# V transposed inside the second projection, the last keys' chain moved into it, and weight loads placed behind x loads, in a one-core hybrid streaming encoder kernel

## The chip, the cores and the metric

The kernel runs on one core of a Trainium2 chip. The metric is the device time of one execution in microseconds (us); lower is better. Engines: TensorE (PE in the profile, its weight loads PEld), VectorE (DVE), ScalarE (ACT), GpSimd (POOL) and SyncE (SP), which here issues nearly all DMAs.

## The reference

One inference step of a two-layer encoder on 2048 prompt tokens and 64 sample tokens, width 1024, in float32:

1. Layer A: x is RMS-normalised and projected to an x branch and a SiLU gate; a causal convolution of width 4, two block-diagonal gates, a linear recurrence over time, the product with the gate, an output projection, and the residual sum x1.
2. Shared keys and values: `kv = rmsnorm(x1) @ w_kv`, 128 columns of keys (2 heads of 64, RMS-normalised per head) and 128 of values.
3. Layer B: x1 is normalised and projected to 1024 query columns (16 heads, RMS-normalised per head) and 1024 gate columns (SiLU). Each chunk of 64 tokens attends to itself and the two chunks before it (the sample: to a cache of 128 tokens and itself), with a learned sink per head. The result times the gate goes through an output projection and is added to x1.

Keys and values of the last 128 tokens, and the convolution's and the recurrence's states, are outputs too.

## The kernel before

**Number format.** Each float32 matmul is three matmuls of rounded operands (high times high, low times high, high times low), so weights and inputs are split into a high part (ACT, `high_part` L906, `high_input` L405) and a low part (`low_part` L911 on DVE or POOL, `low_input` L418 on DVE). Activations lie with features in partitions and tokens in columns.

**Stages.** (a1) first projection, 6 steps of 352 tokens. (recurrent) 8 steps of 264 tokens (RN = 8, RT = 264), each of 4 turns; PE does gates L1432, output projection `out` L1453 (matmul L1465), keys and values L1448, the token sum L1472 and the key sum L1418. (b1) second projection, steps s = 1 to 6 (PN = 6) of PT = 352 tokens, each of 16 slots j of 24 matmuls L791: j < 8 give a block of queries, j >= 8 a block of gates. (attention) a sample tile and 8 tiles of 256 tokens (AN = 8), 8 units each; the first 8 units run inside the last 8 slots of b1 (a `late` slot).

**A slot of b1.** On DVE the block is read out of PSUM (`evacuate`, L691). For a query block ACT squares it (L554) into one of two buffers q2, and DVE adds it to qacc (copy L642 for the first block, sum L645 after), one slot later. After slot 8 PE sums qacc over the heads (`head_sum` L767, matmul L773), and it waits there for the eighth sum (q2_added). The same slots prepare the next step's input: ACT L405 and L412 (square), DVE L418 and L431. In step 1 each slot also splits a weight unit: ACT L906, then POOL L911. SP issues, in the order of the slots, input loads L392, weight loads `load_unit` L843 and the stores of finished gate and query blocks L481 and L485 (`project_sync` L444). Each engine runs its list in order, so whatever is issued behind a waiting instruction waits too.

**What hangs on slots.** `project_sync` has a table of extra work by (step, slot), run at the slot's start: (1,4) `store_memory` L1046, the last K and V blocks to DRAM; (1,12) `store_states` L1584, ten small stores; (PN,0) `start` L1599, which waits for all query stores and loads the sample tile and tile 1 (`tile` L1547); (PN,8) and (PN,10) gate loads; (PN,12) to (PN,15) tile 2.

**The last keys.** The chain for the last 264 tokens runs in b1's first slots: DVE L1256 and L1258 read keys and values out, DVE L1261 squares, PE `key_sum` L1414 (L1418, after slot 0), ACT root L1360, DVE reciprocal L1265 and product L1267. ACT's first square of step 1 waits for that key sum (`r.kms_done`), and so does POOL before `spread_heads` L963 at slot 1. All token and key sums use PSUM bank 5, so `out` blocks 1 and 3 wait for the roots that read it.

**V in attention.** Values are kept with features in partitions, but PE needs them with tokens in partitions. So each tile loads `m.vt` by DMA (L1556, L1557, L1571), and in unit 0 PE transposes it (`transpose_v` L1708: four blocks L1720, then L1722 and L1723), and ACT and DVE copy the result to `m.v` and `m.v_last` (`read_v`, L1963 to L1972 on ACT, L1839 on DVE). The transposes of probabilities (`transpose_p` L1693, matmuls L1702 and L1705) use the same banks 4 and 5 and wait for those copies.

```python
            def head_sum(t):
                eng.wait_ge(m.q2_added, NB * (t + 1))
...
                if i == 0:
                    eng.wait_ge(m.va_done, s + 1)
                    eng.wait_ge(m.vb_done, s + 1)
```

Of the kernel before, what the change touches and what calls it, by code (L numbers as in the profile page):

```python
# [24 lines left out]
P = 128  # L25
D = 1024
# [61 lines left out]
def build(nc, A):  # L88
    stack = ExitStack()
    with stack:  # L90
# [50 lines left out]
        spread_made = sem("spread_made")  # L141
# [21 lines left out]
        def project_memory(tag, heads):  # L163
            with ExitStack() as own:
# [28 lines left out]
                if heads:  # L193
                    b(f"{tag}_gap0", [P, 2048 - 3 * PT])
                    m.q2, m.qacc = b(f"{tag}_q2", [P, 2, PT]), b(f"{tag}_qacc", [P, PT])
                else:
                    m.std = b(f"{tag}_std", [P, PT])
# [19 lines left out]
            if heads:  # L217
                m.late_tanh, m.late_done = sem(f"{tag}_late_tanh"), sem(f"{tag}_late_done")
                m.q2_done, m.q2_added = sem(f"{tag}_q2_done"), sem(f"{tag}_q2_added")
                m.qms_done = sem(f"{tag}_qms_done")  # L220
# [86 lines left out]
        with ExitStack() as own:  # L307
# [24 lines left out]
            m.vt = [b(f"m_vt{i}", [P, WINDOW + AT]) for i in range(2)]  # L332
            m.v = [b(f"m_v{i}", [P, 4, P]) for i in range(2)]
            b("m_gap1", [P, 23 * PT - 7424 + 32])
# [28 lines left out]
        m.vt_done = sem("m_vt_done")  # L363
        m.va_done = sem("m_va_done")
        m.vb_done = sem("m_vb_done")
# [4 lines left out]
        m.v_last_zero = sem("m_v_last_zero")  # L370
# [73 lines left out]
        def project_sync(eng, m, starts):  # L444

            def body(s, par):
                for j in range(2 * NB):
# [20 lines left out]
                    if known(s, 1, PN):  # L468
                        t = s - 1
                        if m.heads and not gate:  # L470
                            continue
# [66 lines left out]
        def project_scalar(eng, m, after):  # L538
            def body(s, par):
# [97 lines left out]
        def add_query(eng, m, t, q):  # L637

            eng.wait_ge(m.q2_done, NB * t + q + 1)
            if q == 0:  # L640
                need(eng, m.qms_done, t)
                nc.vector.tensor_copy(m.qacc[:, :], m.q2[:, 0, :]).then_inc(m.q2_added, 1)  # L642
            else:
                eng.wait_ge(m.q2_added, NB * t + q)
                nc.vector.tensor_tensor(m.qacc[:, :], m.qacc[:, :], m.q2[:, q % 2, :], ALU.add).then_inc(m.q2_added, 1)  # L645
# [120 lines left out]
        def project_tensor(eng, m, after):  # L766
            def head_sum(t):  # L767

                if isinstance(t, int) and t == 0:
                    eng.wait_ge(spread_made, 2)  # L770
# [192 lines left out]
        def spread_heads(eng):  # L963
# [5 lines left out]
              .then_inc(spread_made, 1)  # L969
            eng.wait_ge(spread_made, 1)  # L970
            nc.gpsimd.affine_select(out=spread, in_=spread, compare_op=ALU.is_ge, fill=0.0, base=NB - 1,
                                    pattern=[[NB, P // NB], [0, NB]], channel_multiplier=-1).then_inc(spread_made, 1)
# [40 lines left out]

        EARLY = {(PN, 2): 0, (PN, 6): 1, (PN, 8): 2, (PN, 11): 3, (PN, 13): 4}

# [36 lines left out]
        def recurrent_sync(eng):  # L1052
# [31 lines left out]

            def load_next(pair, q):
# [4 lines left out]
            def body(s, par):  # L1090
                for g in range(NG):
# [79 lines left out]
            for i in range(2):  # L1171
                eng.wait_ge(r.x1_stored[i], 16 * RN * NB // 2)

        def recurrent_vector(eng):
# [73 lines left out]
            def tail_read(t):  # L1248
# [10 lines left out]
                eng.wait_ge(r.kv_read, 2 * t + 1)  # L1259
                need(eng, r.kms_done, t)  # L1260
                nc.vector.tensor_tensor(r.k2[:, :], r.k[:, :], r.k[:, :], ALU.mult).then_inc(r.k2_done, 1)  # L1261

            def tail_norm(t):
                eng.wait_ge(r.kstd_done, t + 1)
                nc.vector.reciprocal(r.std[:, :], r.std[:, :]).then_inc(r.krec_done, 1)  # L1265
                eng.wait_ge(r.krec_done, t + 1)
                nc.vector.scalar_tensor_tensor(out=r.k[:, :], in0=r.k[:, :], scalar=vec[:, KN, 0:1], in1=r.std[:, :],  # L1267
                                               op0=ALU.mult, op1=ALU.mult).then_inc(r.k_done, 1)

            def turn(s, par, g):  # L1270
# [13 lines left out]
                if known(s, 2, RN + 1) and g == 3:  # L1284
                    tail_norm(s - 2)
# [28 lines left out]
            eng.wait_ge(r.x1_free, 1)  # L1314

        def recurrent_scalar(eng):
# [29 lines left out]
            def turn(s, par, g):  # L1346
# [5 lines left out]
                if known(s, 2, RN + 1) and g == 2:  # L1352
                    eng.wait_ge(r.ms_done, t + 1)
                    need(eng, r.k_done, t)
                    nc.scalar.activation(r.std[:, :], bank[5][:, 0:RT], ACT.Sqrt, scale=1.0 / D,
                                         bias=eps[:, 0:1]).then_inc(r.std_done, 1)
                if known(s, 2, RN + 1) and g == 3:
                    eng.wait_ge(r.rstd_done, t + 1)
                    eng.wait_ge(r.kms_done, t + 1)
                    nc.scalar.activation(r.std[:, :], bank[5][:, 0:RT], ACT.Sqrt, scale=1.0 / HEAD,  # L1360
                                         bias=eps[:, 0:1]).then_inc(r.kstd_done, 1)
# [52 lines left out]
        def key_sum(eng, t, last):  # L1414
            eng.wait_ge(r.k2_done, t + 1)
            if not last:
                eng.wait_ge(r.resid_done, NB * (t + 1) + 2)
            nc.tensor.matmul(bank[5][:, 0:RT], head_ones[:, :], r.k2[:, :], start=True, stop=True)\  # L1418
              .then_inc(r.kms_done, 1)

        def recurrent_tensor(eng):
# [31 lines left out]
            def out(t, tp, blk):  # L1453
# [3 lines left out]
                if blk == 1:  # L1457
                    need(eng, r.std_done, t)
                if blk == 3:
# [9 lines left out]
            def token_sum(t):  # L1469
                eng.wait_ge(r.sq_added, NB * (t + 1))  # L1470
                eng.wait_ge(r.resid_done, NB * (t + 1))
                nc.tensor.matmul(bank[5][:, 0:RT], ones[:, :], r.acc[:, :], start=True, stop=True)\  # L1472
# [72 lines left out]

        def attention_sync(eng):
            def tile(s, par, parts=range(4)):  # L1547

                done = m.tile_loaded[par]
                if isinstance(s, int) and s == 0:  # L1550
# [5 lines left out]
                    eng.dma_start(m.vt[0][:, 0:WINDOW], A["v0"]).then_inc(done, 16)  # L1556
                    eng.dma_start(m.vt[0][:, WINDOW:WINDOW + SAMPLE], A["v"][:, 0:SAMPLE]).then_inc(done, 16)  # L1557
# [7 lines left out]
                for part in parts:  # L1565
# [4 lines left out]
                    if part == 1:  # L1570
                        eng.dma_start(m.vt[par][:, w0:w0 + width], A["v"][:, cols(at - WINDOW + w0, width)])\  # L1571
                           .then_inc(done, 16)
# [26 lines left out]
            def start():  # L1599
# [4 lines left out]
                for stored in b1.stored:  # L1604
                    eng.wait_ge(stored, 16 * NB)
                tile(0, 0)
                tile(1, 1)

            def gate_sample():
                eng.wait_ge(b1.proj_done, 2 * NB * (PN - 1) + NB - 1)  # L1610
                tile_gate(0, 0)

            def gate_first():
                eng.wait_ge(b1.qms_done, PN)
                tile_gate(1, 1)
# [17 lines left out]
            project_sync(eng, b1, {(1, 4): lambda: store_memory(eng, RN - 1), (1, 12): store_states, (PN, 0): start,  # L1633
# [32 lines left out]
        def loaded(eng, s, par):  # L1666

            eng.wait_ge(m.tile_loaded[par], s * 56 + (112 if par == 0 else 56))
# [5 lines left out]
        def attention_tensor(eng):  # L1674
# [18 lines left out]
            def transpose_p(s, par, i):  # L1693
# [4 lines left out]
                if i == 0:  # L1698
                    eng.wait_ge(m.va_done, s + 1)
                    eng.wait_ge(m.vb_done, s + 1)  # L1700
# [7 lines left out]
            def transpose_v(s, par):  # L1708

                before = unit_of(s, 0)  # L1710
                need(eng, m.pta_done, before)
                need(eng, m.ptb_done, before)
                loaded(eng, s, par)
                if isinstance(s, int) and s == 0:
# [450 lines left out]
```

## Time and profile before

| | us |
|---|---|
| three runs | 1519.57, 1520.12, 1522.78 |
| their median | 1520.12 |
| profiled execution, device time | 1520.08 |
| span of its profile | 1518.3 |
| PE busy in the span | 1469.9 (97%) |
| DVE, ACT, POOL busy | 1042.4, 709.0, 258.1 |
| mean granted TensorE clock, share of full speed | 0.993 |

The span is the part of the execution that the profile covers, on its only core. A time in a row, such as 774.79, is counted in us from the start of the span. A bracket at the end of a row, as `[4.06 <-ACT m_pt_a L1961]`, says how long the engine had been idle before it and what ended that.

### The profile page before, as it was taken

Reading aid. Unit: us, or ns where it says so; the run is one execution under the profiler, and the core shown is the slowest. Engines: PE = TensorE matmul, PEld = TensorE weight load, DVE = VectorE, ACT = ScalarE, POOL = GpSimd, SP = SyncE. Lnnn points to the kernel's source line nnn. Section 1 sums busy time; section 2 is a strip of 40 time slices with the busy share of each in tenths; the row PEclk is TensorE's granted clock in tenths of the full one; section 3 lists DMA queues with packets and bytes.
Section 4 is the critical chain, followed back from the end, with each engine's and each line's share of the span. In section 5 each row is a group of like instructions: output and inputs, shape, how many; then the busy total and the mean of one; then the engine's idle time right before and its main releaser. Section 6 shows DMA issues by size and latency. Waiting matters only on the chain.

```text
span 1518.3 us, 31662 instructions
## 1 busy us (share of the span) xinstructions
PE 1469.9 (97%) x10668; PEld 1409.0 (93%) x10668; DVE 1042.4 (69%) x2254; ACT 709.0 (47%) x1584; POOL 258.1 (17%) x199
## 2 busy tenths in 40 slices
PE   7999999999999999999899999999988999999999
PEld 7999999999899999998899999999976788878888
DVE  7987866765698888888863453534377877767771
ACT  5432432336887777772352341433335444434440
POOL 0011111101344444341440000000001111111110
PEclk9999999999999999999999999999999999999999
DMA  6565655569855555556522202212264244423312
GB/s 238 169 211 198 219 178 202 198 225 334 280 169 171 153 168 163 160 164 209 161 62 81 96 30 91 77 52 92 64 196 130 80 111 121 121 80 102 96 50 77
DMA packets 202711, 219.35 MB, mean 144 GB/s; under 512 B 60496, under 2 KB 189264, under 8 KB 202576
## 3 DMA queue, kind: packets, MB, share of 16 engines
q1 hardware_dynamic: 190448, 208.27, 43.7%
q10 hardware_dynamic: 12128, 9.39, 1.9%
q8 instruction: 71, 1.16, 0.3%
q14 instruction: 64, 0.52, 0.1%
HBM read 132.56 MB, written 85.30 MB: 143 GB/s over the span
## 4 chain that ended last, share of the span: by engine, by line
PE 62%; DVE 5%; ACT 2%; issue 2%; DMA 1%; SPq 0%; ACTq 0%; POOL 0%; DVEq 0%
PE s_banks L791 22%; PE bank L1754 10%; PE bank L1465 10%; PE s_banks L1432 5%; PE s_banks L1687 3%; PE bank L1448 3%; PE bank L791 2%; PE bank L1702 2%; PE bank L1736 2%; ACT m_p L1950 2%; PE bank L1740 1%; DVE m_nmax L1808 1%; PE bank L1705 1%; DMA r_x<-xT_dram 1%; DMA x_dram<-r_x 1%
## 5 line engine op out<-in xcount | busy, mean ns | idle before, releaser
L1950 ACT ACTIVATE m_p<-s_banks,m_nm 128x192 f32<-128x192 f32 (+2 forms) x264 | 106.1, 414 | 185.8 <-DVE m_nm L1812 185.5
L1754 PE MATMUL bank<-m_y_hi,w_hi_a 128*128 128x256 f32 (+1 forms) x512 | 150.7, 294 | 2.8 <-DVE w_lo_a L911 2.1
L1754 PE MATMUL bank<-m_y_lo,w_hi_a 128*128 128x256 f32 (+1 forms) x512 | 145.6, 284 | 0.0
L1754 PE MATMUL bank<-m_y_hi,w_lo_a 128*128 128x256 f32 (+1 forms) x512 | 145.5, 284 | 0.0
L791 PE MATMUL bank<-a_hi,w_hi_a 128*128 128x352 f32 x384 | 123.7, 322 | 1.3 <-DVE a_out L691 1.1
L791 PE MATMUL bank<-a_hi,w_lo_a 128*128 128x352 f32 x384 | 124.0, 323 | 0.0
L791 PE MATMUL bank<-a_lo,w_hi_a 128*128 128x352 f32 x384 | 123.9, 323 | 0.0
L791 PE MATMUL s_banks<-b_hi,w_hi_b 128*128 128x352 f32 x336 | 110.8, 330 | 0.0
L1465 PE MATMUL bank<-r_y_hi,w_hi_a 128*128 128x264 f32 x384 | 109.3, 285 | 0.6 <-ACT r_std L1360 0.6
L1465 PE MATMUL bank<-r_y_lo,w_hi_a 128*128 128x264 f32 x384 | 109.1, 284 | 0.0
L1465 PE MATMUL bank<-r_y_hi,w_lo_a 128*128 128x264 f32 x384 | 108.9, 283 | 0.0
L791 PE MATMUL s_banks<-b_hi,w_lo_b 128*128 128x352 f32 x336 | 108.8, 324 | 0.0
L791 PE MATMUL s_banks<-b_lo,w_hi_b 128*128 128x352 f32 x336 | 108.1, 322 | 0.0
L2007 POOL TENSOR_TENSOR m_y_lo<-m_y,m_y_hi 128x256 fp32r<-128x256 f32 x66 | 48.6, 736 | 349.1 <-DVE m_y_hi L1865 349.1
L578 ACT ACTIVATE a_out_hi<-a_out 128x352 fp32r<-128x352 f32 (+1 forms) x48 | 23.9, 498 | 172.8 <-DVE a_out L745 172.8
L791 PE MATMUL s_banks<-b_hi,w_hi_a 128*128 128x352 f32 x320 | 104.1, 325 | 0.0
L791 PE MATMUL s_banks<-b_hi,w_lo_a 128*128 128x352 f32 x320 | 103.3, 323 | 0.0
L791 PE MATMUL s_banks<-b_lo,w_hi_a 128*128 128x352 f32 x320 | 103.2, 323 | 0.0
L1754 PEld LDWEIGHTS bank<-m_y_hi,w_hi_a 128*128 128x128 f32 x512 | 96.7, 189 | 4.8 <-DVE w_lo_a L911 3.9
L1754 PEld LDWEIGHTS bank<-m_y_lo,w_hi_a 128*128 128x128 f32 x512 | 97.4, 190 | 0.0
L1754 PEld LDWEIGHTS bank<-m_y_hi,w_lo_a 128*128 128x128 f32 x512 | 97.3, 190 | 0.0
L791 PE MATMUL bank<-a_hi,w_hi_b 128*128 128x352 f32 x288 | 93.3, 324 | 0.3 <-DVE a_out L691 0.3
(224 smaller groups left out, 4624.3 us busy)
## 6 DMA issues: line engine op xcount, KB each, us to landing
w_raw_b<-weights_dram SPq DMA_DIRECT2D x26, 512.0 KB, 4.6
w_raw_a<-weights_dram SPq DMA_DIRECT2D x25, 512.0 KB, 4.6
sga_dram<-a_out SPq DMA_DIRECT2D x48, 176.0 KB, 2.9
r_xc_hi<-xc_hi_dram SPq DMA_DIRECT2D x32, 264.0 KB, 3.0
r_xc_lo<-xc_lo_dram SPq DMA_DIRECT2D x32, 264.0 KB, 3.3
r_xc<-xc_dram SPq DMA_DIRECT2D x32, 264.0 KB, 3.8
r_sg<-sga_dram SPq DMA_DIRECT2D x32, 264.0 KB, 3.6
r_x<-xT_dram SPq DMA_DIRECT2D x64, 132.0 KB, 2.1
```

Source lines behind the costliest of these rows:

```text
L578: nc.scalar.activation(m.out_hi[:, q, 0:width], m.out[:, place(m, j), 0:width], ACT.Copy)\
L791: mm = nc.tensor.matmul(project_bank(m, s, j)[:, 0:PT], w[pw][:, kt * P:(kt + 1) * P], x[:, kt, :], start=(n == 0), stop=(n == 3 * NB - 1))
L1432: mm = nc.tensor.matmul(bank[2 * mat + ob][:, 0:RT], w[pw][:, at:at + P], x[px][:, q, kt, :].bitcast(F32R), start=(i == 0), stop=(i == 5))
L1448: mm = nc.tensor.matmul(bank[6 + o][:, 0:RT], w[pw][:, blk * P:(blk + 1) * P], (r.x1_hi, r.x1_lo)[px][:, blk % 2, :], start=(blk == 0 and ...
L1465: mm = nc.tensor.matmul(bank[4 + blk % 2][:, 0:RT], w[pw][:, kt * P:(kt + 1) * P], (r.y_hi, r.y_lo)[px][tp][:, kt, :], start=(i == 0), sto ...
L1687: mm = nc.tensor.matmul(s_banks[:, 2 * (i % 2) + e, bp * 192 + v0:(bp + 1) * 192], m.q[par][rows, j, blk:blk + 2, :].rearrange("p b t -> p ...
L1702: nc.tensor.transpose(bank[4][:, k * P:(k + 1) * P], m.p[:, i % 2, k, 0:P], ident[:, :])
L1705: mm = nc.tensor.transpose(bank[5][:, e * P:(e + 1) * P], last, ident[:, :])
L1736: nc.tensor.matmul(bank[6][e * HEAD:(e + 1) * HEAD, 0:AT], m.v[par][:, j, n * HEAD:(n + 1) * HEAD], m.pt_a[:, e * AT:(e + 1) * AT], start= ...
L1754: mm = nc.tensor.matmul(out_bank(ts, blk)[:, 0:width], w[pw][:, kt * P:(kt + 1) * P], (m.y_hi, m.y_lo)[px][tp][:, kt, 0:width], start=(n = ...
L1950: nc.scalar.activation(m.p[:, q, k, v0:192], s_banks[:, 2 * q + e, bp * 192 + v0:(bp + 1) * 192], ACT.Exp, bias=m.nm[:, q, k:k + 1], accum ...
L2007: nc.gpsimd.tensor_tensor(y_part(m.y_lo, s, par, i), m.y[:, q, :, :], y_part(m.y_hi, s, par, i).bitcast(F32), ALU.subtract).then_inc(m.y_l ...
```

## The change

1. **V is transposed in b1.** V is cut into 18 blocks of up to 128 tokens: the cached one in step 1, four in each of steps 2 to 5, the last 64 tokens in step 6. A block takes four slots: SP reads it (64 KB) into one buffer `v_in`, PE transposes it after the next slot's matmuls (`turn`), ACT copies it to `v_out` in the third, SP writes it to a new DRAM scratch `vt` in the fourth. Steps 2 to 5 do this in slots 4i to 4i+3, step 1 in slots 12 to 15, step 6 in slots 0 to 3. `read_turn` and `write_turn` stand at the end of a slot's work on SP.
2. **Attention reads rows of `vt`.** `m.vt`, `transpose_v`, both `read_v` and the waits on them go. Instead SP loads `m.v` (`values_rows`, 1 to 3 DMAs a tile) and `m.v_last` (`last_rows`, 2 a tile). `start` waits until 17 blocks are written, before its first load; `gate_first` waits for all 18. POOL's memsets are in more pieces.
3. **One q2 buffer.** ACT's square of block j waits for DVE's sum of block j-1; before, of block j-2. ACT's wait on the last key sum goes.
4. **The last keys' chain is spread:** DVE squares after slot 0, PE sums and ACT takes the root after slot 2 (bank 7), DVE reciprocal and product after slot 3, `store_memory` at (1,6). POOL's wait for the key sum stays, ahead of `spread_heads`.
5. **Two sums in free banks.** The token sum of the seventh recurrent block (RN - 2) goes to bank 2 and its key sum to bank 3, so the last `out` no longer waits for the roots.
6. **Weight loads behind x loads.** At recurrent turn (RN, 0), SP issues weight units 1 and 2 of b1 behind the first x load and 3 and 4 behind the second, not all four ahead of both.

```diff
@@ project_sync
+                    else:
+                        read_turn(eng, s, j)
+                        write_turn(eng, s, j)
@@ project_scalar
-                            need(eng, m.q2_added, NB * t + j - 1)
-                            if j == 0 and isinstance(s, int) and s == 1:
-                                eng.wait_ge(r.kms_done, RN)
-                            nc.scalar.activation(m.q2[:, j % 2, :], m.q[:, j, :], ACT.Square)\
-                              .then_inc(m.q2_done, 1)
+                            need(eng, m.q2_added, NB * t + j)
+                            nc.scalar.activation(m.q2[:, :], m.q[:, j, :], ACT.Square).then_inc(m.q2_done, 1)
@@ recurrent_sync
+            def gates_free(s, g, first):
+                if isinstance(s, int) and (s, g) == (RN, 0):
+                    for k in (first, first + 1):
+                        load_unit(eng, U_B1 + k, r.gates_done, 4 * NG * RN)
...
-                    if isinstance(s, int) and (s, g) == (RN, 0):
-                        for k in range(1, 1 + UNITS_GATE):
-                            load_unit(eng, U_B1 + k, r.gates_done, 4 * NG * RN)
...
                     if behind:
                         load_x(behind, 0)
+                    gates_free(s, g, 1)
...
                         load_x(behind, 1)
+                    gates_free(s, g, 3)
@@ recurrent_tensor
-                if blk == 1:
+                if blk == 1 and not last_sums(t - 1):
                     need(eng, r.std_done, t)
-                if blk == 3:
+                if blk == 3 and not last_sums(t - 1):
                     need(eng, r.kstd_done, t)
@@ attention_sync and b1
+        def read_turn(eng, s, j):
+            for i in turns(s, j, 0):
+                n, width = turned(s, i), turn_width(s)
+                need(eng, b1.v_turned, n)
...
+                eng.dma_start(b1.v_in[:, 0:width], src).then_inc(b1.v_read, 16)
+        def turn(eng, s, j):
+            for i in turns(s, j, 1):
+                n, width = turned(s, i), turn_width(s)
+                eng.wait_ge(b1.v_read, n * 16 + 16)
+                need(eng, b1.v_copied, n)
...
+                nc.tensor.transpose(bank[5][0:width, 0:P], b1.v_in[:, 0:width], ident[:, :]).then_inc(b1.v_turned, 1)
+        def copy_turn(eng, s, j):
+            for i in turns(s, j, 2):
...
+                nc.scalar.activation(b1.v_out[0:width, :], bank[5][0:width, 0:P], ACT.Copy).then_inc(b1.v_copied, 1)
+        def write_turn(eng, s, j):
+            for i in turns(s, j, 3):
...
+                eng.dma_start(dst, b1.v_out[0:width, :]).then_inc(b1.v_written, 16)
@@ start
+                eng.wait_ge(b1.v_written, 16 * (4 * (PN - 2) + 1))
                 tile(0, 0)
+                values_rows(0, 0)
                 tile(1, 1)
@@ attention_tensor
-                if i == 0:
-                    transpose_v(s, par)
             def after_queries(s, j):
-                if isinstance(s, int) and (s, j) == (1, 0):
+                turn(eng, s, j)
+                if isinstance(s, int) and (s, j) == (1, 2):
                     key_sum(eng, RN - 1, True)
@@ attention_scalar, unit
-                if i == 0:
-                    read_v(s, par)
```

## Rows read from the trace of the kernel before

**Rows 1.** PE's waits: releaser, us in total, times, longest us.

```profile
PE bank L1448 <- DVE r_x_lo L1233: 8.0, 4, 3.2
PE bank L1720 <- ACT m_pt_a L1961: 7.0, 3, 4.1
...
PE bank L1702 <- ACT m_v_last L1972: 2.7, 5, 0.7
...
PE bank L1465 <- ACT r_std L1360: 0.6, 1, 0.6
...
PE bank L1465 <- ACT r_std L1355: 0.6, 1, 0.6
```

**Rows 2.** PE's timeline, two waits for x: start us, us, instruction [idle].

```profile
697.50 0.39 PE L1448 MATMUL bank<-r_x_hi,w_hi_a 128*128 128x264 f32 x1 [1.61 <-DVE r_x_lo L1233]
...
735.37 0.52 PE L1448 MATMUL bank<-r_x_hi,w_hi_a 128*128 128x264 f32 x1 [3.22 <-DVE r_x_lo L1233]
```

**Rows 3.** The chain that ended last: start us, us, what.

```profile
686.70 7.00 DMA x_dram<-r_x
```

**Rows 4.** PE's timeline at the first head_sum.

```profile
774.79 0.76 PE L773 MATMUL bank<-b_qacc,head_ones 128*128 128x352 f32 x2
```

**Rows 5.** DVE's timeline in b1's step 1.

```profile
746.86 1.16 DVE L1267 SCALAR_TENSOR_TENSOR r_k<-r_k,vec,r_std 128x264 f32<-128x264 f32 x1
...
764.03 1.48 DVE L645 TENSOR_TENSOR b_qacc<-b_qacc,b_q 128x352 f32<-128x352 f32 x1
...
773.99 0.51 DVE L645 TENSOR_TENSOR b_qacc<-b_qacc,b_q 128x352 f32<-128x352 f32 x1
```

**Rows 6.** POOL's timeline in the same stretch.

```profile
744.49 0.40 POOL L967 TENSOR_SCALAR_AFFINE_SELECT head_ones<-ones 128x128 f32<-128x128 f32 x1 [1.14 <-PE bank L1418]
...
745.33 7.30 POOL L911 TENSOR_TENSOR w_lo_b<-w_raw_b,w_hi_b 128x1024 fp32r<-128x1024 f32 x3
...
762.73 2.40 POOL L911 TENSOR_TENSOR w_lo_a<-w_raw_a,w_hi_a 128x1024 fp32r<-128x1024 f32 x1 [1.41 <-ACT w_hi_a L906]
```

**Rows 7.** SP's timeline in the same stretch.

```profile
743.43 7.25 SPq L843 DMA_DIRECT2D w_raw_a<-weights_dram  x3
```

**Rows 8.** ACT's timeline, a slot of the same stretch.

```profile
764.15 0.50 ACT L554 ACTIVATE b_q<-b_q 128x352 f32<-128x352 f32 x1 [1.50 <-DVE b_q L691]
...
765.42 1.04 ACT L906 ACTIVATE w_hi_a<-w_raw_a 128x1024 fp32r<-128x1024 f32 x1
```

**Rows 9.** DMA view: KB each, median us from issue to landing.

```profile
sgb_dram<-b_out SPq DMA_DIRECT2D x48, 176.0 KB, 1.9
...
m_q<-qn_dram SPq DMA_DIRECT2D x33, 256.0 KB, 4.4
...
m_k<-k_dram SPq DMA_DIRECT2D x2, 64.0 KB, 2.6
```

**Rows 10.** SP's timeline in slot 12 of step 2.

```profile
855.80 0.98 SPq L485 DMA_DIRECT2D qn_dram<-b_q  x2
```

**Rows 11.** PE's timeline at the end of slot 13 of step 2.

```profile
857.44 0.32 PE L791 MATMUL s_banks<-b_hi,w_hi_a 128*128 128x352 f32 x1
```

**Rows 12.** SP's timeline around slot 12 of step 1.

```profile
789.70 0.45 SPq L1587 DMA_DIRECT2D conv_sample_dram<-halo_sample  x1
...
798.47 0.46 SPq L481 DMA_DIRECT2D sgb_dram<-b_out  x1
```

**Rows 13.** PE's timeline at the end of slot 13 of step 1.

```profile
794.60 0.32 PE L791 MATMUL s_banks<-b_hi,w_hi_a 128*128 128x352 f32 x1
```

**Rows 14.** SP's timeline in `start`, step 6 slot 0.

```profile
1063.09 3.66 SPq L1574 DMA_DIRECT2D m_q<-qn_dram  x4
```

**Rows 15.** PE's timeline at the end of slot 1 of step 6.

```profile
1061.99 0.32 PE L791 MATMUL s_banks<-b_hi,w_hi_b 128*128 128x352 f32 x1
```

**Rows 16.** Windows: busy us by engine (instructions), granted clock, DMA share, GB/s.

```profile
1140.00:1163.00 23.00, 16.70 (x131) 11.69 (x128) 17.75 (x49) 14.75 (x52) 2.89 (x4) 0.85 0.35 114
```

**Rows 17.** PE's timeline, V's transposes in slot 10 of step 6.

```profile
1107.82 1.12 PE L1720 MATMUL bank<-ident,m_vt 128*128 128x128 f32 x4 [4.06 <-ACT m_pt_a L1961]
```

More of the change, by code:

```diff
@@ L219, in project_memory @@
                 m.q2_done, m.q2_added = sem(f"{tag}_q2_done"), sem(f"{tag}_q2_added")
+                m.v_read, m.v_turned, m.v_copied, m.v_written = (sem(f"{tag}_v_{k}") for k in ("read", "turned", "copied", "written"))
                 m.qms_done = sem(f"{tag}_qms_done")
@@ L467, in body @@
                         load_unit(eng, m.unit + 10 + j)
-                    if known(s, 1, PN):
+                    if known(s, 1, PN) and not (m.heads and not gate):
                         t = s - 1
-                        if m.heads and not gate:
-                            continue
                         if late(m, s, j):
@@ L1172, in recurrent_sync, with key_square, key_norm @@
                 eng.wait_ge(r.x1_stored[i], 16 * RN * NB // 2)
+        def key_square(eng, t):
+            eng.wait_ge(r.kv_read, 2 * t + 1)
+            need(eng, r.kms_done, t)
+            nc.vector.tensor_tensor(r.k2[:, :], r.k[:, :], r.k[:, :], ALU.mult).then_inc(r.k2_done, 1)
+        def key_norm(eng, t):
+            eng.wait_ge(r.kstd_done, t + 1)
+            nc.vector.reciprocal(r.std[:, :], r.std[:, :]).then_inc(r.krec_done, 1)
+            eng.wait_ge(r.krec_done, t + 1)
+            nc.vector.scalar_tensor_tensor(out=r.k[:, :], in0=r.k[:, :], scalar=vec[:, KN, 0:1], in1=r.std[:, :],
+                                           op0=ALU.mult, op1=ALU.mult).then_inc(r.k_done, 1)
         def recurrent_vector(eng):
@@ L1258, in tail_read @@
                 nc.vector.tensor_tensor(r.v[:, :], bank[7][:, 0:RT], r.rstd[:, :], ALU.mult).then_inc(r.kv_read, 1)
[L1259 to L1268, printed above, removed]
+                if not (isinstance(t, int) and t == RN - 1):
+                    key_square(eng, t)
             def turn(s, par, g):
@@ L1314, in recurrent_vector, with key_root @@
             eng.wait_ge(r.x1_free, 1)
+        def key_root(eng, t):
+            eng.wait_ge(r.rstd_done, t + 1)
+            eng.wait_ge(r.kms_done, t + 1)
+            nc.scalar.activation(r.std[:, :], bank[key_bank(t)][:, 0:RT], ACT.Sqrt, scale=1.0 / HEAD,
+                                 bias=eps[:, 0:1]).then_inc(r.kstd_done, 1)
         def recurrent_scalar(eng):
@@ L1415, in key_sum @@
             eng.wait_ge(r.k2_done, t + 1)
-            if not last:
+            if last:
+                eng.wait_ge(r.kv_read, 2 * RN)
+            elif last_sums(t):
+                eng.wait_ge(r.gates_read, 4 * NG * RN)
+            else:
                 eng.wait_ge(r.resid_done, NB * (t + 1) + 2)
-            nc.tensor.matmul(bank[5][:, 0:RT], head_ones[:, :], r.k2[:, :], start=True, stop=True)\
+            nc.tensor.matmul(bank[key_bank(t)][:, 0:RT], head_ones[:, :], r.k2[:, :], start=True, stop=True)\
               .then_inc(r.kms_done, 1)
@@ L1544, in out_block, with turns, turned @@
             return (s - 1, i - 2) if known(s, 2, LAST - 1) else None
-        def attention_sync(eng):
+        def turns(s, j, step):
+            if not isinstance(s, int):
+                return [j // 4] if j % 4 == step else []
+            if s == 1:
+                return [3] if j == 12 + step else []
+            return [0] if s == PN and j == step else []
+        def turned(s, i):
+            if isinstance(s, int):
+                return 0 if s == 1 else 4 * (PN - 2) + 1
+            return s * 4 + (i - 7)
@@ L1706, in transpose_p @@
                 mm.then_inc(m.t_done, 1)
[L1708 to L1714, printed above, removed]
-                    eng.wait_ge(b1.std_done, PN)
-                if isinstance(s, int) and s == 1:
-                    eng.wait_ge(m.v_zero, 1)
-                pairs = 2 if isinstance(s, int) and s == 0 else 5
-                for k in range(min(pairs, 4)):
-                    nc.tensor.transpose(bank[4][:, k * P:(k + 1) * P], m.vt[par][:, k * CHUNK:k * CHUNK + P], ident[:, :])
-                k = pairs - 1
-                nc.tensor.transpose(bank[5][:, 0:P], m.vt[par][:, k * CHUNK:k * CHUNK + P], ident[:, :])
-                nc.tensor.transpose(bank[5][0:HEAD, P:2 * P], m.vt[par][:, pairs * CHUNK:(pairs + 1) * CHUNK], ident[:, :])\
-                  .then_inc(m.vt_done, 1)
             def values(s, par, i):
```

158 lines of the change are left out of this document (93 added, 65 removed).

## The prediction

> **What bounds the kernel now.** Four views, in this order. The table's busy times: PE works 1469.9 of 1518.3 us, so about 48 us can be won at most and each new PE wait is paid in full. The list of PE's waits: few are long; those that the change aims at are x landing before L1448, the two roots before L1465, and V's transposes with what follows them [rows 1]. PE's timeline at the first of them, a wait of 1.61 [rows 2], and the chain of waits ahead of it: the x load stood behind an x store of 7.00 us, into which the four weight loads fell [rows 3]. Last the timelines by engine at each place where the new work is put; a cover shows there as time between what SP or DVE does and what PE does next.
>
> The sum is made against the profiled execution, 1520.08 us (span 1518.3), 0.04 below the median of 1520.12. About 0.2%, 3 us, is what a measurement of this kernel can tell from no change.
>
> **Recurrent stage (parts 5 and 6).** The waits it can remove are 1.61 for x, 0.6 and 0.6 for roots [rows 1, 2], 2.8 in all. What is late next is the second x load: its wait of 3.22 stands right before b1 [rows 2], so much of what is won earlier is waited for there. The weight loads come later by as much. I take -1.2 (0 to -2.8).
>
> **Last keys and one q2 buffer (parts 3 and 4): the first head_sum.** Before, it ran at 774.79, right behind the last sum, which DVE ended at 774.50 [rows 4, 5]: 0.3 us to spare. Three things make that sum late.
> - POOL stood still until the key sum and ran its last small piece from 744.49 [rows 6]. That sum now comes two slots of 3.84 later less the time that is no longer waited for, about 750.8. So POOL's weight splits, 2.4 us each (7.30 for three [rows 6]), run unbroken to about 763.9 instead of to 757.7. SP's weight loads of that stretch, which need the buffers free [rows 7], and the input loads behind them slide by 6 us too.
> - DVE does the key product and reciprocal (3 us, the product ending at 748.0 before [rows 5]) after slot 3, in the middle of the queries.
> - While POOL runs a split, DVE sums wait: the sum at 764.03 took 1.48 where the one at 773.99 took 0.51, and the first ended 0.38 behind POOL's split of 762.73 [rows 5, 6]. With both together I get DVE reading block 4 out at 766.6, about 6.8 late.
> - With one buffer the square waits for the sum of the block before. From a square's start to POOL's next split are 2.3 us (764.15 to 766.46 [rows 8]); DVE comes to its next sum at the same moment or later, finds POOL at work for 2.40, and the next square waits for that sum: 2.3 + 2.4 + 0.4 and small gaps = 5.2 us a slot against PE's 3.84.
> - So the eighth sum ends at 766.6 + 3 x 5.2 + 3.3 = 785.5, head_sum starts at 785.8: +11.2. Lower bound: no slide of DVE, only the one-buffer loop, +5; if the loop doesn't form either, about +0.3; upper bound +14. The key sum's own wait ahead of it goes, inside this wait.
>
> **V's blocks (part 1).** 18 transposes of 0.12 us in PE's flow (four take 0.5 when nothing is in their way): +2.2. Else they cost what PE waits for the read. A read is at the end of slot 4i's work on SP, PE wants it after slot 4i+1. For 64 KB the rows show 2.6 us to landing, for 176 KB 1.9 [rows 9]; I take 2.0 where the queues are quiet. The Trainium skill ("DMA: Bandwidth & Descriptors", section on the anatomy of one DMA) gives 2.0 us fixed plus bytes over 436 GB/s, an estimate of 2.15 for 64 KB, measured there on GpSimd's path and not SP's; the two medians lie on both sides of it, and by it the term for steps 2 to 5 would be 7.4.
> - *Slot 13 of steps 2 to 5.* SP leaves slot 12's stores at 855.80 + 0.98 = 856.78 [rows 10], so the read goes at 857.1 and lands at 859.1; PE is ready at 857.44 [rows 11]. 1.6 each, +6.4 (0.9 to 2.3 each). Slots 1, 5 and 9 come out with nothing to wait: SP is a slot ahead there.
> - *Slot 13 of step 1.* `store_states` puts ten DMAs ahead, from 789.70; SP is free for the read at 798.47 [rows 12]. In that crowd landings take longer: between the medians of 1.9 and 4.4 [rows 9] I take 3.4, so 801.9. PE is ready at 794.5 [rows 13]: +7.4 (5 to 8).
> - *Slot 1 of step 6.* The read is behind the whole of `start`, whose last q load is issued at about 1065.4 and, at 4.4 us to landing, lands near 1070 [rows 9, 14]. `start` now first waits for the write of block 17 (+2), and there is one more V load. The read lands about 1072.8; PE is ready at 1061.9 [rows 15]: +10.9 (8 to 12).
> - *Cold clock.* Behind a wait of 3.22 the first matmul took 0.52 against 0.39 [rows 2] and some 1.5 us are lost before the granted clock is at full level (2.4 GHz) again; 23 us that hold long PE gaps show 0.85 [rows 16]. I add 1.4 behind each of the three long waits (11.2, 7.4, 10.9): 4.2.
>
> Other steps of the move: the write (64 KB) costs SP about 0.4 in a slot of 3.84 and nobody waits for it but `start`; ACT's copy, about 0.4, lies in slack of ACT (47% busy), and if that were gone the gate's activation would be late. Attention's six or so loads a tile replace one or two on SP, which has time there. `gate_sample` goes one slot later, with two slots before its first reader.
>
> **What attention gets back.** 51 transposes go (6 a tile). Waits: V's transpose for ACT, 7.0 in three, of which 4.06 in slot 10 [rows 1, 17]; of that one ACT and DVE's work for the next unit stays, and some clock and slow transposes are won besides: 4.5. Tile 2: of 2.5, 1.6. The sample's unit 0.7, tile 3 1.9. Tiles 4 to 7: 0.66 of transposes and about 0.5 of the wait for the last copy (2.7 in five [rows 1]), 1.15 each, 4.6; tile 8 0.9. Together -14.2 (-8 to -17).
>
> **Sum.** -1.2 + (11.2 + 1.4) + (7.4 + 1.4) + 6.4 + (10.9 + 1.4) + 2.2 - 14.2 = +26.9: 1547.0 us.
>
> **Rivals.**
> - *Head_sum in time.* If DVE's next sum comes a hair before POOL's split, or POOL catches up, no loop forms. For: both are within 0.1 us in my working. Against: POOL's 2.4 and DVE's 1.4 of such work fill 3.8 of 3.84, so lateness once there isn't made up. 1547.0 - 12.6 = 1534.4. With the loop but no late start (+5) 1540.8; that belongs to the forecast's own spread. Chance 0.2.
> - *SP is free when the reads come, the faster side.* If SP gets to slots 12 and 0 earlier, or the reads overtake the loads ahead of them, no turn waits: 1547.0 - 8.8 - 6.4 - 12.3 = 1519.5, no difference. It decides for faster if also head_sum stays at its +5 and the gains reach their ends: 1520.1 - 2.8 + 5 + 2.2 - 17 = 1507.5; the point is reads issued 2 us before PE is ready. Against: SP's rows give times after PE's in three places. Chance 0.1, half of it faster.
> - *Worse.* Reads of 512-byte rows and writes lie in queues with input loads: 2.6 to landing in all steps (+4), slots 1, 5 and 9 also late by a few tenths (+4), head_sum +14: 1558. Chance 0.1.
> - *The change does not do what it says.* V's work doesn't leave attention's rhythm, since DVE and ACT keep the pace there: gain -8, 1553. It lies in the range.
>
> **How the numbers follow.** Forecast with its own spread 0.6, head_sum in time 0.2, SP free 0.1, worse 0.1. Range 1528 to 1557: it leaves out the third case and the end of the fourth. Faster 0.06, same 0.05, slower 0.89.
>
> **What would show it.** In the list of PE's waits: L773 behind DVE L645, about 11; the new transpose behind the DMA of v_in, six waits: about 7 near 805, 11 near 1085, four of 1.6. The sum's rows in step 1 at 5.2 us apart. V's transposes gone from attention, with L1736 and L1754 following the probabilities without the copy's wait. In the recurrent stage no wait of L1465 for a root. Wrong would be: no wait at L773; turns that wait under 0.5; attention shorter by less than 8.

## The result, and the profile after

The kernel after takes 1547.97 us (median of four runs, 1547.47 to 1551.41) against 1520.65 before (four runs): the ratio is 1.0186, 95% interval 1.0168 to 1.0204. The forecast was 1547.0.

The profiled execution of the kernel after took 1551.41 us, 3.4 above its median, so the sums below, made against the profiled 1520.08 of before, have 31.3 us to explain and not the 27.3 between the medians. The page of the kernel after, span, busy times and the granted clock in 40 slices:

```profile
span 1549.7 us, 31791 instructions
...
PE 1468.2 (95%) x10634; PEld 1407.1 (91%) x10634; DVE 1031.6 (67%) x2235; ACT 700.8 (45%) x1577; POOL 258.9 (17%) x203
...
PEclk9999999999999999999979999999899999999999
```

PE has as much work as before and the span grew, so the answer is in waits. PE's waits in the kernel after (releaser, us in total, times, longest us):

```profile
PE bank L1608 <- DMA b_v_in<-v_dram: 24.5, 6, 10.6
PE bank L770 <- DVE b_qacc L642: 14.0, 1, 14.0
...
PE bank L1469 <- DVE r_x_lo L1255: 8.5, 5, 3.1
PE bank L1827 <- ACT m_pt_a L2036: 7.1, 5, 2.2
```

Two lines are new: 24.5 us in six waits for V blocks, and 14.0 at the first head_sum (L770 is L773 of before). The wait for x, which parts 5 and 6 aim at, didn't shrink (8.0 before, [rows 1]). The waits of L1720 and L1702 in [rows 1] have no counterpart: those transposes and copies are gone. L1827 is L1736 of before, which waited 4.1 in four; part of what V's transposes waited for in tile 2 is now waited for there.

Where the 31.3 us lie, from the starts of b1's first matmul, of the six head_sums and of attention's first and last output matmul in both timelines:

| stretch | forecast | before | after | change |
|---|---|---|---|---|
| to b1's start | -1.2 | 737.29 | 739.28 | +2.0 |
| to the first head_sum | +11.2 | 37.50 | 50.81 | +13.3 |
| to the second (slot 13 of step 1, cold clock twice) | +10.6 | 62.85 | 74.73 | +11.9 |
| to the fifth | +6.2 | 188.54 | 196.54 | +8.0 |
| to the sixth (slot 13, then slot 1 of step 6) | +14.3 | 62.85 | 77.30 | +14.5 |
| from there to the last output matmul | -14.2 | 426.05 | 407.68 | -18.4 |
| sum | +26.9 | | | +31.3 |

**The first head_sum.** DVE's timeline in the kernel after, step 1 of b1 (some of before's lines are in [rows 5]):

```profile
757.11 0.53 DVE L688 TENSOR_TENSOR b_q<-s_banks,b_std 128x352 f32<-128x352 f32 x1 [3.14 <-PE s_banks L788]
757.55 1.79 DVE L642 TENSOR_TENSOR b_qacc<-b_qacc,b_q 128x352 f32<-128x352 f32 x1
763.94 2.76 DVE L417 SCALAR_TENSOR_TENSOR b_lo<-b_x,vec,b_hi 128x352 fp32r<-128x352 f32 x1 [4.60 <-ACT b_hi L404]
766.62 2.53 DVE L427 COPY b_acc<-b_sq 128x352 f32<-128x352 f32 x1
769.07 1.79 DVE L1191 RECIPROCAL r_std<-r_std 128x264 f32<-128x264 f32 x1
770.90 0.49 DVE L1193 SCALAR_TENSOR_TENSOR r_k<-r_k,vec,r_std 128x264 f32<-128x264 f32 x1
771.31 0.52 DVE L688 TENSOR_TENSOR b_q<-s_banks,b_std 128x352 f32<-128x352 f32 x1
...
774.30 0.52 DVE L688 TENSOR_TENSOR b_q<-s_banks,b_std 128x352 f32<-128x352 f32 x1
...
777.79 2.66 DVE L430 TENSOR_TENSOR b_acc<-b_acc,b_sq 128x352 f32<-128x352 f32 x1
780.38 0.51 DVE L688 TENSOR_TENSOR b_q<-s_banks,b_std 128x352 f32<-128x352 f32 x1
...
783.36 0.52 DVE L688 TENSOR_TENSOR b_q<-s_banks,b_std 128x352 f32<-128x352 f32 x1
...
786.82 2.69 DVE L430 TENSOR_TENSOR b_acc<-b_acc,b_sq 128x352 f32<-128x352 f32 x1
789.43 0.51 DVE L642 TENSOR_TENSOR b_qacc<-b_qacc,b_q 128x352 f32<-128x352 f32 x1
```

POOL's timeline there, against [rows 6], and SP's, against [rows 7]:

```profile
753.27 0.40 POOL L964 TENSOR_SCALAR_AFFINE_SELECT head_ones<-ones 128x128 f32<-128x128 f32 x1 [8.00 <-PE bank L1439]
...
754.20 7.39 POOL L908 TENSOR_TENSOR w_lo_b<-w_raw_b,w_hi_b 128x1024 fp32r<-128x1024 f32 x3
761.55 2.41 POOL L908 TENSOR_TENSOR b_w_lo<-b_w_raw,b_w_hi 128x1024 fp32r<-128x1024 f32 x1
763.92 5.03 POOL L908 TENSOR_TENSOR w_lo_a<-w_raw_a,w_hi_a 128x1024 fp32r<-128x1024 f32 x2
...
777.73 2.34 POOL L908 TENSOR_TENSOR w_lo_a<-w_raw_a,w_hi_a 128x1024 fp32r<-128x1024 f32 x1 [0.25 <-ACT w_hi_a L903]
```

```profile
745.34 14.02 SPq L840 DMA_DIRECT2D w_raw_a<-weights_dram  x3
759.53 14.78 SPq L391 DMA_DIRECT2D b_x<-x_dram  x6
```

The lines of before for the first input, for the read of block 4 and for the input loads:

```profile
758.04 0.57 DVE L418 SCALAR_TENSOR_TENSOR b_lo<-b_x,vec,b_hi 128x352 fp32r<-128x352 f32 x1
...
759.77 0.52 DVE L691 TENSOR_TENSOR b_q<-s_banks,b_std 128x352 f32<-128x352 f32 x1 [0.91 <-PE s_banks L791]
```

```profile
750.85 1.75 SPq L392 DMA_DIRECT2D b_x<-x_dram  x4
```

POOL stood still for 8.00 us (1.14 before), SP's three weight loads stretch over 14.02 us (7.25 before) because they need buffers that POOL still reads, the input loads start at 759.53 and not at 750.85, and DVE gets its first input of the next step at 763.94 and not at 758.04. By then POOL runs without a break until 768.95, and DVE's copy of 0.33 takes 2.53. The last key's reciprocal and product follow, and block 4 is read out at 771.31 and not at 759.77. After that the blocks come 2.99, 6.08 and 2.98 us apart. The long slots hold one sum of the next input's squares (L430) of 2.66 or 2.69 us, which stands beside a split on POOL; where POOL is idle the same sum takes 0.52.

**The reads of V.** PE's timeline at three of the six waits in the kernel after (the first fence), and SP's (the second):

```profile
820.47 0.48 PE L1608 MATMUL bank<-ident,b_v_in 128*128 128x128 f32 x1 [7.67 <-DMA b_v_in<-v_dram]
...
953.49 0.33 PE L1608 MATMUL bank<-ident,b_v_in 128*128 128x128 f32 x1 [1.43 <-DMA b_v_in<-v_dram]
...
1109.99 0.42 PE L1608 MATMUL bank<-ident,b_v_in 128*64 128x128 f32 x1 [10.63 <-DMA b_v_in<-v_dram]
```

```profile
807.65 0.45 SPq L1689 DMA_DIRECT2D conv_sample_dram<-halo_sample  x1
...
815.62 0.40 SPq L1599 DMA_DIRECT2D b_v_in<-v_dram  x1
...
1096.15 0.40 SPq L1654 DMA_DIRECT2D m_q<-qn_dram  x1
...
1103.02 2.98 SPq L1676 DMA_DIRECT2D m_q<-qn_dram  x4
1106.05 1.44 SPq L1599 DMA_DIRECT2D b_v_in<-v_dram  x1
```

The reads stand behind the ten stores that begin at 807.65 and behind all of `start`. The source view of L1599 gives their time to landing:

```profile
DMA to landing us min/median/max: 1.8/1.9/4.8
```

**The clock.** Windows of the kernel after (busy us of each engine, then granted clock, DMA share, GB/s):

```profile
741.00:776.00 35.00, 35.00 (x217) 34.53 (x215) 19.58 (x22) 8.26 (x16) 21.14 (x11) 1.00 0.31 98
776.00:791.00 15.00, 1.01 (x4) 0.69 (x3) 12.44 (x14) 8.19 (x14) 8.89 (x4) 0.59 0.13 37
791.00:812.00 21.00, 21.00 (x118) 20.75 (x117) 9.16 (x16) 9.59 (x15) 4.79 (x2) 0.88 0.25 71
```

Before the wait the mean granted clock is 1.00 (2.4 GHz), in it 0.59, and in the 21 us behind it, in which PE never pauses, 0.88: the clock was at its lower level (1.2 GHz) for a part of each. At full clock 24 matmuls take 3.84 us; the 118 of this window took 21.0 instead of 18.9, 2.1 us.

### The profile page after: what moved, and what is told of

The parts are those of the page before. It is cut to its first block, busy times and chain, and to the rows that moved or that the text cites. A ratio compares the mean times of both kernels' runs of the same rounds, so it can differ in the third digit from the quotient of the medians.

```text
span 1549.7 us, 31791 instructions
## 1 busy us (share of the span) xinstructions
PE 1468.2 (95%) x10634; PEld 1407.1 (91%) x10634; DVE 1031.6 (67%) x2235; ACT 700.8 (45%) x1577; POOL 258.9 (17%) x203
## 4 chain that ended last, share of the span: by engine, by line
PE 58%; DVE 5%; DMA 4%; ACT 2%; issue 2%; SPq 2%; POOL 0%; DVEq 0%; ACTq 0%
PE s_banks L788 19%; PE bank L1845 11%; PE bank L1486 9%; PE s_banks L1453 5%; PE s_banks L1795 3%; PE bank L1469 2%; PE bank L1810 2%; PE bank L1827 2%; DMA x_dram<-r_x 2%; PE bank L788 2%; PE bank L1831 2%; ACT m_p L2025 1%; DMA b_v_in<-v_dram 1%; DVE m_nmax L1898 1%; PE bank L1813 1%
## 5 line engine op out<-in xcount | busy, mean ns | idle before, releaser
L788 PE MATMUL s_banks<-b_hi,w_hi_a 128*128 128x352 f32 x320 | 107.5, 336 | 0.0
```

What stands on the lines that cost most here:

```text
L788: mm = nc.tensor.matmul(project_bank(m, s, j)[:, 0:PT], w[pw][:, kt * P:(kt + 1) * P], x[:, kt, :], start=(n == 0), stop=(n == 3 * NB - 1))
```

## The experiments

Ratios are to the kernel before, timed on the same chip. All edits are made to the kernel after.

**All reads at the start of their slots.**

```diff
                 gate, blk = part(m, j)
+                if m.heads:
+                    read_turn(eng, s, j)
                 if isinstance(s, int) and (s, j) in starts:
...
                 else:
-                    read_turn(eng, s, j)
                     write_turn(eng, s, j)
```

> Each read of a V block is issued at the start of its slot, ahead of store_states, of start and of the stores of the slot. Theory (the turns wait because the read stands behind other work on SP): the 24.5 us that PE waits in six places for v_in fall under 1, and the cold clock behind the waits of 7.7 and 10.6 us goes too: 1548 - 24.5 - 5 = about 1518. Rival (the landing itself is slow, or the work behind the reads becomes late instead): a wait of over 1 us stays at each turn, or a new one appears at the attention's first loads, and the time stays above 1528.

Measured: 1516.97 us, ratio 0.9968 (0.9955 to 0.9980), already 0.3% faster than before. PE's waits in this kernel:

```profile
PE bank L771 <- DVE b_qacc L643: 12.0, 1, 12.0
PE bank L789 <- DVE a_w_lo L909: 10.1, 1, 10.1
PE bank L1470 <- DVE r_x_lo L1256: 9.1, 4, 3.3
```

No wait for a V block is left, and SP's other work behind the reads makes nobody late. The rival is out.

**The reads of one place each.** The same edit, for step 1 alone, for step 6 alone, and for steps 2 to 5 alone.

> Only step 1's read of a V block is issued at the start of its slot, ahead of the ten stores of store_states. Theory (each turn's wait is a fault of its own place on SP): the 7.7 at slot 13 of step 1 goes, with about 1.6 of cold clock; but the next waits stay: 1548 - 9.3 = about 1538.7. Rival (the waits are linked, a later one takes up what an earlier one gives): the turns of step 2 or 6 wait longer by some us and the time is above 1543.

> Only step 6's read is issued at the start of its slot, ahead of start and its loads. Theory: the 10.6 in slot 1 of step 6 goes with 1.6 of cold clock, but the first attention units find their loads less far ahead: about 1536 if those loads were in time, which the kernel before had at the same distance. Rival: the attention's first units wait for loads instead, 1540 or more.

> Only the sixteen reads of steps 2 to 5 are issued at the start of their slots. Theory: the four waits of 1.4 to 2.0 in slot 13 go, 6.2 in all, with little cold clock: about 1541. Rival (a read at the slot's start waits for its buffer and holds the stores behind it): new waits for stores, 1546 or more.

Measured: 1537.73 (ratio 1.0102, 1.0086 to 1.0119), 1533.43 (1.0092, 1.0070 to 1.0113) and 1540.52 (1.0129, 1.0112 to 1.0145). Against 1547.97 they win 10.2, 14.5 and 7.5, together 32.2, where all at once won 31.0 (by the ratios to before, which leave out what the chips differ in, some 12.8, 14.3 and 8.7, together 36, for 33). The timelines are sharper: the stretches of the table that hold an edit's own reads are 10.2, 12.6 and 8.8 shorter than in the kernel after, together 31.6, and with all reads early the way from the first head_sum to the sixth is 31.6 shorter too. So these are three faults of their own, nothing linked. Step 6's edit won 2.3 more than the 12.2 that I had forecast, but its own stretch fell by 12.6 (77.30 to 64.75), so what is above that isn't its doing. The wait lists: for step 1's edit 17.1 in five are left, for step 6's 13.1 in five, for the middle one's 19.0 in two:

```profile
PE bank L1611 <- DMA b_v_in<-v_dram: 17.1, 5, 11.3
```

```profile
PE bank L1611 <- DMA b_v_in<-v_dram: 13.1, 5, 7.4
```

```profile
PE bank L1611 <- DMA b_v_in<-v_dram: 19.0, 2, 11.4
```

**The last keys' chain back at its old places**, with one q2 buffer as in the kernel after.

```diff
-                if not (isinstance(t, int) and t == RN - 1):
-                    key_square(eng, t)
+                key_square(eng, t)
...
-                if known(s, 2, RN) and g == 3:
+                if known(s, 2, RN + 1) and g == 3:
                     key_norm(eng, s - 2)
...
-                if isinstance(s, int) and (s, j) == (1, 2):
+                if isinstance(s, int) and (s, j) == (1, 0):
                     key_sum(eng, RN - 1, True)
...
-            project_sync(eng, b1, {(1, 6): lambda: store_memory
+            project_sync(eng, b1, {(1, 4): lambda: store_memory
```

> The last keys' chain is back at its old places (square with the reading out, sum after slot 0, root before the first square, product before the queries, store_memory at slot 4); everything else, the one q2 buffer too, as in the changed kernel. Theory (lateness of POOL and DVE at the start of step 1 makes the eighth sum late, and the one buffer adds some 5): the wait of 14.0 at the first head_sum falls to about 5, less 0.9 for the key sum's wait that returns: about 1540. Rival (the one buffer alone makes the loop): the wait stays at 10 or more and the time at 1545 or more.

**POOL not held by the key sum.**

```diff
-                        if j == 1:
+                        if j == 5:
                             spread_heads(eng)
```

> POOL makes spread_ones after slot 5's split and not after slot 1's, so it doesn't stand still for the last key sum; the chain stays late. Theory (POOL's 8.0 us of standing still is the larger part): its splits end some 8 us earlier, the input loads are back in time, and the wait at the first head_sum falls from 14.0 to 5 to 7: about 1540. Rival (the key product in the middle of the queries on DVE, or the one buffer, is what counts): the wait stays at 10 or more.

**Two squares in turn**, with the chain late as in the kernel after.

```diff
-                            need(eng, m.q2_added, NB * t + j)
-                            nc.scalar.activation(m.q2[:, :], m.q[:, j, :], ACT.Square)
+                            need(eng, m.q2_added, NB * t + j - 1)
+                            if j == 1:
+                                need(eng, m.q_normed, NB * t)
+                            nc.scalar.activation(square_of(m, j), m.q[:, j, :], ACT.Square)
```

> ACT's squares alternate between two buffers again (the second is the tensor of the heads' roots, free in those slots), the chain stays late. Theory (lateness plus POOL's and DVE's turn-taking): the wait of 14.0 falls by 2 at most, time 1546 to 1548. Rival (the one buffer makes the loop): it falls to 6 or less, about 1540. In steps 2 to 6 no change under either.

Measured: the chain back 1538.34 (ratio 1.0115, 1.0091 to 1.0139), POOL free 1541.42 (1.0131, 1.0109 to 1.0153), two squares 1545.73 (1.0158, 1.0134 to 1.0183). Their waits at the first head_sum, in the same order:

```profile
PE bank L770 <- DVE b_qacc L642: 3.8, 1, 3.8
```

```profile
PE bank L770 <- DVE b_qacc L642: 6.6, 1, 6.6
```

```profile
PE bank L776 <- DVE b_qacc L648: 11.0, 1, 11.0
```

So POOL's standing still is the largest single part: letting it go on takes 14.0 to 6.6, though the chain is as late as in the kernel after. The rest of the chain's lateness costs the next 2.8, from 6.6 to 3.8; I read that as its product amid DVE's query work, which no run takes by itself. What is left with the chain back, 3.8, is the one buffer's: from b1's start to the first head_sum that kernel takes 41.58 us, the kernel before 37.50, and the next one below, with two buffers as well, 37.42. These weights are good to some 2 us, because this wait swings where nothing in its stretch differs: it was 14.0 in the kernel after and with step 1's reads early, and 12.0 in the three other kernels with early reads. Two buffers without the rest win little: 11.0 against 12.0 to 14.0, so 1 to 3, where I had expected 2 at most.

**Three edits together**, reads early, chain back, two squares; then the same with the weight loads of part 6 ahead of the x loads again, with the sums of part 5 back in bank 5, and with both.

> Three edits together on the changed kernel: reads of V blocks at the start of their slot, the last keys' chain at its old places, two buffers for the squares. Theory (the 14.0 at head_sum and the 24.5 at the turns are two separate faults, each with a cold clock behind it, and the attention keeps its gain of 18): from the 1517.0 of the kernel with early reads go 12.0 of waiting and about 2 of cold clock, so about 1503, 1.1% faster than before. Rival (V's work in b1 costs in other ways once these waits are gone): above 1508.

> As f1_mended, and the four weight loads stand ahead of the x loads again. Theory (the x wait of 1.6 that the move wins comes back as a later wait for x, since SP is held in the last turns anyway): no difference to f1_mended beyond 1.5 us, b1 starts within 1 us of it. Rival (the loads moved back cost b1's start): f1_mended is faster by 2 or more, or slower by 2 or more.

> As f1_mended, and the last token and key sums but one use bank 5 again, with out's two waits for the roots. Theory: the two waits of 0.6 come back, and PE, 1.2 later, waits that much less for the last x: no difference to f1_mended beyond 1 us. Rival (the two waits are paid in full): 1.2 slower.

> As f1_mended with both undone, so the recurrent stage is issued as in the kernel before. Theory: b1 starts at 737.3 as there, and the time is within 1.5 us of f1_mended. Rival: the two edits add up to 2 us or more, one way or the other.

| kernel | us | ratio to before | b1 starts at (one profile) |
|---|---|---|---|
| three edits | 1505.58 | 0.9896 (0.9879 to 0.9912) | 739.53 |
| and loads back | 1504.00 | 0.9878 (0.9860 to 0.9896) | 741.57 |
| and sums back | 1503.46 | 0.9886 (0.9870 to 0.9903) | 738.05 |
| and both back | 1503.34 | 0.9882 (0.9866 to 0.9899) | 736.49 |
| both back, once more | 1502.19 | 0.9887 (0.9870 to 0.9903) | 736.75 |

All five beat the kernel before by 1.0 to 1.2% (the intervals reach down to 0.9), and the kernel after by more. Among themselves the intervals overlap, so the times don't settle whether parts 5 and 6 cost something; that they win nothing that can be measured is plain. My expectations missed in detail: the kernels with the sums back and with both back are 2.1 and 2.2 us below the three edits, where I expected 1 and 1.5 at most, and with the loads back b1 started 2.0 later and not within 1. One profile each is little for such a difference. Counted from an output matmul ahead of all that parts 5 and 6 touch (678.10 in the kernel before, 678.98 in the kernel after), b1 starts 58.8 to 59.2 us later in the three profiles with neither part (before and the two with both back), and 59.1 to 61.6 later, 60.1 on average, in the nine with both. By that the two parts cost about 1 us. The waits of the kernel with both back hold neither new line:

```profile
PE bank L795 <- DVE a_w_lo L915: 9.8, 1, 9.8
PE bank L1475 <- DVE r_x_lo L1262: 6.9, 4, 3.1
PE bank L1833 <- ACT m_pt_a L2038: 5.9, 5, 2.1
```

**That kernel once more**, for the pace of attention's units.

> f4_mended_both_back once more, unchanged, for the pace of the attention's units: its profile showed 5.51 us a unit throughout, that of the changed kernel 5.42, those of other kernels one pace before the pause in the middle and the other behind it. Theory (the pace belongs to an execution, not to a kernel): a second profile can show 5.42 in one or both halves. Rival (it belongs to the kernel): 5.51 in both again. One profile that shows 5.51 again would settle nothing. The time again near 1503.

The source view of the output matmul, in the window from 1250 to 1262 us (durations min/median/max in ns), of the first execution of this kernel and of this second one, and then the second's from 1400 to 1412 us:

```profile
L1851 PE MATMUL bank<-m_y_hi,w_hi_a x18: 281/281/364, 1250.3 to 1261.8; 128*128 128x256 f32 x18
```

```profile
L1851 PE MATMUL bank<-m_y_hi,w_hi_a x19: 275/277/368, 1250.2 to 1261.8; 128*128 128x256 f32 x19
...
L1851 PE MATMUL bank<-m_y_hi,w_hi_a x16: 280/282/365, 1401.7 to 1409.7; 128*128 128x256 f32 x16
```

The same program ran its units at 5.51 us all the way in one execution, and at 5.42 up to the pause in the middle and 5.51 behind it in the other. The rival is out: the pace belongs to the execution.

## Why the prediction was right, step by step

**The time** came out at 1547.97 for 1547.0, and that it is so close is luck. The sum was +26.9 against the profiled executions' +31.3: the clock, the head_sum, the recurrent stage were put too low and V's transposes and attention's gain were off the other way, and the profiled execution of the kernel after was itself 3.4 above its median. The direction, the places and the size of the waits are not luck.

**Reads of V: right, in place and in size.** Six waits were forecast with 24.7 us (7.4, four of 1.6, 10.9); six came, with 24.5 (7.67, 2.00, three of 1.40 to 1.43, 10.63). Slots 1, 5 and 9 waited for nothing, as said. In step 1 the landing took 4.8 (815.62 to 820.43) where I took 3.4, and SP came to it 2.8 behind PE where I took 4.0. The median landing was 1.9 where I took 2.0. The estimate of 2.15 from the Trainium skill ("DMA: Bandwidth & Descriptors", anatomy of one DMA) lies above that median, and the measurement decides. (The 7.4 that I gave for steps 2 to 5 by it should have been 7.0, 0.15 more for each of four.)

**The first head_sum: the place and the mechanism right, the amount mis-sized by 2.** I forecast +11.2 (my own working, 785.8 less 774.79, gives 11.0) and the stretch grew by 13.3. Of the chain of steps, POOL's late start and the slide of SP's loads were right in kind, but the key sum came at 753.2 and not at 750.8 (b1 itself began 2.0 later), the input at 763.9, and two DVE operations ran into POOL's splits one after the other; so block 4 was read out at 771.3 and not at 766.6. The loop of 5.2 us a slot did not form as I had it: DVE and POOL took turns, a short slot of 3.0 and a long one of 6.1, 4.5 on average, and what waited for POOL was the sum of the next input's squares (L430), not the sum of the queries that I had named, which kept its 0.52. The two errors have opposite signs. Taken away in turn, the causes weigh 5.4 to 7.4 (POOL), 2.8 (the rest of the chain) and 3.8 (the one buffer, for which alone I had said 5).

That DVE and POOL exclude each other is in the rows: a copy of 0.33 us took 2.53 and ended 0.20 behind POOL's split, and a sum of 0.52 at 757.55 took 1.79 while POOL ran. The read of block 3 out of PSUM, L688 at 757.11, ran beside the same split and kept its 0.53. The Trainium skill ("SBUF — State Buffer", section on SBUF's two separate sides) states that a GpSimd operation, and a VectorE one in a 2-port mode or with two inputs in SBUF, hold the shared port pair for the whole instruction, whichever starts first, and that the other is blocked; the trace agrees.

**Cold clock: too low, and the transposes too high.** I took 1.4 behind each of three long waits, from a wait of 3.22 [rows 2], 4.2 in all. Behind the 14.0 it was 2.1 and more, and early reads with their head_sum wait of 12.0 show the step after it at 64.95 instead of 62.85, 2.1. From the first head_sum to the sixth the kernel after takes 348.6 us and the kernel before 314.2. The six waits are 24.5 of these 34.4; V's 18 transposes are 0.5, since the kernels with three edits, which have the transposes and none of the waits, take 314.7. So 9.3 is left for what the waits cost beyond themselves, and the 2.2 for the transposes is a term that the runs show at 0.5.

**Recurrent stage: wrong in sign.** I took -1.2 and it was +2.0 in this profile, of which 0.9 had already come by 678, ahead of the first instruction that parts 5 and 6 touch; the rest, 1.1, lies in the stretch that they touch. The step that failed is the one that said what is won early is only partly waited for again later. The waits by place, in the two timelines: of before 1.61 at 696 and 0.57 and 0.63 for the roots are gone or down to 0.30; in their place are 1.72 at 706 and 2.16 at 731 where 0.45 was. In SP's timeline two weight loads now stand at 689.5 and two at 696.0, between x loads, and the wait comes at a later one. The runs with parts 5 and 6 undone show them to win nothing, and the nine profiles with them to cost about 1.

**Attention: mis-sized.** I forecast -14.2, and -18.4 was measured. The units at a tile's start, 6.17 and 6.07 us before, have the length of the others, as forecast, and in place of the wait of 4.06 [rows 17] there is one of 1.01. What I had no term for is the pace of all other units: 5.51 in most of the profile of before and 5.42 in that of after, 0.09 for each of some 37 units, 3.4 us. The last experiment shows it to be no effect of the change, so the change's own gain is about 15, by subtraction. (The trace of before has 52 transposes of V, not the 51 of my sum.)

**The rivals.** Head_sum in time did not happen; after the chain's edit alone 3.8 is left. SP free when the reads come is what early reads made of it: 1516.97 where this rival said 1519.5. Its faster end, 1507.5, is passed by the kernels that have head_sum mended as well. The worse case was wrong in slots 1, 5 and 9, which waited for nothing, and the one in which attention keeps its rhythm fell with the gain of 15.

## What to carry to other kernels

Work that is moved into free time of one engine has to be placed on every queue that it passes: here PE's 18 transposes cost 0.5 us, and the reads for them 31, all of which went by issuing each read one slot's work earlier. Before an engine's wait is moved to a later event, ask what else stands behind that wait: POOL's one wait for a key sum held the splits, these the weight loads, these the input loads, and these the sum that PE needed. A chain at the edge of a stage that has 0.3 us to spare is not a free place.

## What the runs showed that I had not expected

The same 24 output matmuls of a unit run in 3.00 us or in 2.91 us, steadily; the granted clock reads full in both. The pace changed at the pause in the middle of attention, and in the kernel before also at the start of two tiles, behind waits of PE of 0.45 and 0.12 us. The source view of the kernel before, 1225 to 1252 us, and of the kernel after, 1270 to 1297 us:

```profile
L1754 PE MATMUL bank<-m_y_hi,w_hi_a x40: 281/281/364, 1226.9 to 1251.5; 128*128 128x256 f32 x40
```

```profile
L1845 PE MATMUL bank<-m_y_hi,w_hi_a x40: 276/276/367, 1272.4 to 1296.5; 128*128 128x256 f32 x40
```

In the fourteen profiles taken (before, after and twelve experiments) the pace was 5.51 in most of before and throughout in four others, 5.42 throughout in three, and in the other six 5.42 ahead of the pause and 5.51 behind it. What sets it is open. It moves the time less than 0.09 times 45 units, 4 us: in the thirteen profiles with the changed attention, the way from the sixth head_sum to the last output matmul took 409.3 to 409.8 us in the four at 5.51 throughout, and 407.0 to 407.7 in all others. One thing works against it: in the three at 5.42 throughout the granted clock fell to its lower level at the pause (0.79 from 1372 to 1388 us in the kernel after), and in the four at 5.51 it stayed full there (1.00 from 1358 to 1374 us with the chain back). Some 2 us between executions is still more than parts 5 and 6 make.
